# Whole projection units and copied head sums in a woven attention, and a reordered expert loop, in an fp32 two-block transformer

## The chip, the cores and the metric

The kernel runs on one core of one Trainium2 chip. The metric is the device time of one execution in microseconds (us), lower is better. TensorE (PE), VectorE (DVE), ScalarE (ACT) and GpSimd (POOL) each run an instruction stream of their own, SyncE (SP) issues most of the loads; they meet at semaphores only, which the program waits on by hand.

## The reference, cut to what matters

Two transformer blocks follow each other on 1024 tokens of width 1024, all in fp32. The parts that the change touches are the attention of the first block and the expert feed-forward of the second:

```
# first block: 8 heads of 64, three dilated windows mixed
q = rms_norm(q per head, g_q) * 64 ** -0.5
k = rms_norm(k per head, g_k)
y_attn = dilated_mixture(q, k, v)      # causal, scores + a bias, exp, sum, times v
y_conv = gb * short_conv(gc * u, conv_w)
...
# second block: 16 experts, each picks its 130 best tokens of 1040
xs  = u[top_idx]                                            # gather
hid = silu(xs @ w_gate[e]) * (xs @ w_up[e])                 # 1024 -> 512
y   = (hid @ w_down[e]) * top_aff                           # 512 -> 1024
out[top_idx] += y                                           # scatter with add
```

## The kernel before, in words

**First attention.** Heads are handled as four pairs `pp` (0 to 3). For a pair the 1024 queries are 8 tiles of 128; tile t needs one chunk of up to 512 keys (t < 4) or two, so a pair has 12 steps `s`: steps 0 to 3 are tiles 0 to 3, steps 4 and 5 tile 4, and so on to steps 10 and 11 for tile 7. At a step `g = 12 pp + s` PE issues `scores(g + 2)` (two heads, up to 512 columns each), `turn_probs(g, 0)` and `turn_probs(g, 1)` (transposes of the exponentials, up to four for each head), `turn_recips(g - 1)` (one transpose, for a tile's first chunk only) and `values(g - 1)`. DVE takes the turned probabilities of head 0 out of PSUM, adds the bias to the scores and takes the minimum (`scores`), and ACT takes those of head 1, does the exponentials and copies the turned reciprocals (`spread_recips`), on which `values` waits.

Between these PE has the projections of the next pair to do, woven in as units of 24 matmuls of 512 columns (`unit(kind, pp, half, part)`, L1273): at steps 0 and 1 the two halves of k, at 2 and 3 of q, 4 and 5 of v, 6 and 7 of u, then c and b. Pair 0 has no unit at steps 6 and 7, the last pair none from step 6. A unit has two parts of 12 matmuls. All kinds share PSUM banks 2 (half 0) and 3 (half 1), so a unit may start when its bank has been read out (`wait_taken`). The same two banks take the head sums of the squares of k (end of step 3) and of q (end of step 5): `head_sums`, L1288. ACT then reads these banks with a square root (`root_halves`, L793, after an exchange of tables, because it does exponentials in between), and DVE divides (`norm_half`, L1007 and L1009: at steps 4 and 5 for k, 6 and 7 for q). So the v unit of step 4 and the u unit of step 6 wait for ACT's square roots.

```
# wait_taken, before: what the unit behind the head sums waits for
elif before in ("ks", "qs"):
    pe.wait_ge(S["a1_sd"], 2 * norm_index(before[0], of) + half + 1)
```

**Experts.** For each of 16 experts PE multiplies the turned tokens `xsT` by four blocks of `w_gate` and `w_up` (L2838), ACT applies silu, DVE the product (`hidT`, L2389); PE multiplies `hidT` by `w_down` (L2846), DVE copies the result to `yT`; PE turns it back (`yT`, `y_rest`, L543), DVE and ACT weigh it (`y_row_a` L2401, `y_row_b` L1977), POOL scatters it with an add (L1656). Between down and the turning back PE turns the next expert's gathered tokens (`turn_tokens`), which DVE takes out to `xsT` (L2382). The order is written out by hand; the middle experts run in a hardware loop (`Fori`). POOL's loop is gather(e + 1), then scatter(e); SP loads each weight block of the next expert when the block before it has been used.

Of the kernel before, what the change touches and what calls it, by code (L numbers as in the profile page):

```python
# [9 lines left out]
ALU = mybir.AluOpType  # L10
# [140 lines left out]
def build(nc, A, out):  # L151

    ctx = ExitStack()
    with ctx:
# [217 lines left out]
        def thirds(t):  # L372
# [22 lines left out]
            a1_u a1_raw a1_sq a1_ss a1_sd a1_r a1_qn a1_vf a1_vt a1_vs a1_s a1_max a1_e a1_t a1_pt_d a1_pt_a a1_o a1_y a1_rd a1_rl a1_rt a1_rb a1_acc  # L395
# [222 lines left out]
        def wait_taken(pe, kind, pp, half):  # L618
# [4 lines left out]
            elif before in ("ks", "qs"):  # L623
                pe.wait_ge(S["a1_sd"], 2 * norm_index(before[0], of) + half + 1)
# [64 lines left out]
        with nc.Block() as block:  # L689
# [58 lines left out]
            def _(act):  # L748
# [39 lines left out]
                def root_halves(kind, pp, first):  # L788

                    i = norm_index(kind, pp)  # L790
                    for half in range(2):
                        act.wait_ge(S["a1_ss"], 2 * i + 2 if i % 2 else 2 * i + half + 1)
                        act.activation(roots[i % 2][:, half * BANK:(half + 1) * BANK], bank(first + half), ACT.Sqrt, scale=1.0 / HD, bias=eps[:, :]).then_inc(S["a1_sd"], 1)  # L793
# [180 lines left out]
            def _(dve):  # L974
# [25 lines left out]

                def norm_half(kind, pp, half):
# [118 lines left out]
                for g in range(DCT * NS):  # L1120
# [121 lines left out]
            def _(pe):  # L1242
# [254 lines left out]
        with nc.Block() as block:  # L1497
# [99 lines left out]
            def _(pool):  # L1597
# [51 lines left out]
                def scatter(e):  # L1649
# [3 lines left out]
                    for r, (ready, n, to, done) in enumerate((("ex_ra", e * 2 + 2, h_rows, "ex_add_a"), ("ex_rb", e + 1, h_pieces, "ex_add_b"))):  # L1653
                        pool.wait_ge(S[ready], n + CREDIT)
# [9 lines left out]
                with pool.Fori(0, NE - 1) as e:  # L1664
                    pool.wait_ge(S["ex_xt"], e * 3 + 3)
                    gather(e + 1)
                    scatter(e)
# [4 lines left out]
            def _(act):  # L1672
# [294 lines left out]
                act.sem_inc(S["ex_rb"], CREDIT)  # L1967
                with act.Fori(0, NE) as e:
                    for j in range(EK):
                        act.wait_ge(S["ex_g"], e * EK + j + 1)  # L1970
                        act.wait_ge(S["ex_h"], e * EK + j - 1 + 2 * CREDIT)
                        act.activation(silu_e[j % 2][:, :], bank(3 + 2 * (j % 2), CAP), ACT.Silu).then_inc(S["ex_s"], 1)
# [4 lines left out]
                    act.activation(y_row[1][:, :], bank(7, P, 0, PIECES), ACT.Copy, scale=weight[1][:, bass.ds(e, 1)]).then_inc(S["ex_rb"], 1)  # L1977

# [8 lines left out]
            def _(dve):  # L1987
                for n in ("aa_max", "aa_y", "mg_ma", "ex_ra"):
                    dve.sem_inc(S[n], CREDIT)
# [395 lines left out]
                def expert(e, more):  # L2385
                    for j in range(EK):
                        dve.wait_ge(S["ex_s"], e * EK + j + 1)
                        dve.wait_ge(S["ex_u"], e * EK + j + 1)
                        dve.tensor_tensor(hidT[:, j, :], silu_e[j % 2][:, :], bank(4 + 2 * (j % 2), CAP), ALU.mult).then_inc(S["ex_h"], 1)  # L2389
# [5 lines left out]
                    if more:  # L2395
                        take_tokens(e + 1)

                    dve.wait_ge(S["ex_free"], e + CREDIT)
                    for n in range(2):
                        dve.wait_ge(S["ex_r"], e * 3 + n + 2)  # L2400
                        dve.tensor_scalar(y_row[0][:, n * BANK:(n + 1) * BANK], bank(5 + n), weight[0][:, bass.ds(e, 1)], None, ALU.mult).then_inc(S["ex_ra"], 1)  # L2401

                take_tokens(0)
                with dve.Fori(0, NE - 1) as e:
                    expert(e, True)
                expert(NE - 1, False)
# [10 lines left out]
            def _(pe):  # L2417
# [410 lines left out]
                def expert(e, more):  # L2828
                    pe.wait_ge(S["ex_xc"], e * 4 + 4)
                    for j in range(EK):  # L2830
                        if j == 1:
                            pe.wait_ge(S["ex_ra"], e * 2 + CREDIT)
                        if j >= 2:
                            pe.wait_ge(S["ex_h"], e * EK + j - 1 + 2 * CREDIT)
                        for w, b, ld, done in ((w_gate, 3, gate_ld, "ex_g"), (w_up, 4, up_ld, "ex_u")):
                            pe.wait_ge(ld[j], 16 * e + 16)
                            for c in range(KD):
                                last = mm(bank(b + 2 * (j % 2), CAP), w[:, j, c, :], xsT[:, c, :], start=(c == 0), stop=(c == KD - 1))  # L2838
                            last.then_inc(S[done], 1)
                    pe.wait_ge(S["ex_h"], e * EK + EK + 2 * CREDIT)  # L2840
                    pe.wait_ge(S["ex_rb"], e + CREDIT)
# [7 lines left out]
                    if more:  # L2849
                        turn_tokens(e + 1)  # L2850

                    pe.wait_ge(S["ex_yt"], e * 4 + 4)
                    turn(bank(7, P, 0, PIECES), y_rest.rearrange("p c n -> p (c n)")).then_inc(S["ex_r"], 1)
                    for n in range(2):
                        for c in range(4):
                            last = turn(bank(5 + n, P, c * P), yT[:, 4 * n + c, 0:P])
                        last.then_inc(S["ex_r"], 1)
# [62 lines left out]
```

## Time and profile before

| | us |
|---|---|
| median of 3 runs (lowest, highest) | 3569.82 (3563.36, 3573.26) |
| the profiled execution | 3568.07 |
| its span, first to last instruction | 3566.2 |
| PE busy (matmuls) | 3323.8, 93% |
| DVE, ACT, POOL busy | 1402.9, 1033.7, 802.4 |
| mean granted clock of TensorE | 0.967 of full speed |

The profile is of one execution. PE is the engine to watch: the others are busy for less than half of the span. A row names line, engine, operation, `out<-in`, the shape, and in brackets how long the engine sat idle before it and what ended that. PEld is the loading of PE's weights, which runs ahead of its matmuls. An fp32 matmul stands in the trace as two, so a `x16` there is eight instructions.

### The profile page before, as it was taken

How to read it: one execution, taken by the hardware profiler on the slowest of the kernel's cores; microseconds unless marked ns; L12 is line 12 of the kernel's file. 1: busy time of each engine (PE TensorE's matmuls, PEld its weight loads, DVE VectorE, ACT ScalarE, POOL GpSimd, SP SyncE). 2: the span in 40 equal slices, each digit the busy share in tenths (PEclk: the TensorE clock that was granted, in tenths of full speed). 3: DMA queues.
4: the chain of work that ended last, by engine and by line, in shares of the span. 5: the costliest groups of instructions: out<-in, count | busy, mean ns of one | idle time of the engine just before them, and what ended most of it. 6: DMA issues, size and time to landing. Idle time of an engine off the chain costs nothing.

```text
span 3566.2 us, 52694 instructions
## 1 busy us (share of the span) xinstructions
PE 3323.8 (93%) x20576; PEld 2909.0 (82%) x20576; DVE 1402.9 (39%) x2466; ACT 1033.7 (29%) x1888; POOL 802.4 (22%) x513
## 2 busy tenths in 40 slices
PE   7999988999999998999999799899999999689996
PEld 5666766888887887998989689898889999589995
DVE  4544553000002544666666630355455043522222
ACT  4433331000001213555555520155445110301112
POOL 3111123333332333122111133110000223012221
PEclk9999999999999998999999999999999999889998
DMA  3100012111112112000000001300000121468886
GB/s 147 30 30 28 27 72 84 47 47 47 47 47 89 48 53 90 19 19 25 19 19 19 13 26 45 108 25 25 21 23 19 64 101 50 167 225 297 294 305 230
DMA packets 75335, 275.44 MB, mean 77 GB/s; under 512 B 10736, under 2 KB 15600, under 8 KB 74400
## 3 DMA queue, kind: packets, MB, share of 16 engines
q1 hardware_dynamic: 67952, 234.08, 19.1%
q0 software_dynamic: 5632, 17.04, 1.9%
q10 hardware_dynamic: 1584, 22.07, 1.5%
q8 instruction: 108, 1.77, 0.2%
q14 instruction: 59, 0.48, 0.0%
HBM read 229.49 MB, written 38.34 MB: 75 GB/s over the span
## 4 chain that ended last, share of the span: by engine, by line
PE 53%; DVE 3%; issue 3%; ACT 1%; DMA 1%; POOL 0%; SPq 0%; DVEq 0%; ACTq 0%; POOLq 0%
PE PS L555 13%; PE PS L2838 7%; PE PS L2434 6%; PE PS L543 5%; PE PS L2498 3%; PE PS L2846 3%; PE PS L2620 3%; PE PS L2696 3%; PE PS L2465 3%; PE PS L2661 3%; PE PS L2499 0%; PE PS L2778 0%; PE PS L2697 0%; DMA part_b<-raw_b 0%; PE PS L2644 0%
## 5 line engine op out<-in xcount | busy, mean ns | idle before, releaser
L577 POOL CAST w_hi<-ring 128x1024 fp32r<-128x1024 f32 x174 | 183.9, 1057 | 1929.4 <-PE PS L555 772.6
L579 POOL TENSOR_TENSOR w_lo<-ring,w_hi 128x1024 fp32r<-128x1024 f32 x174 | 435.5, 2503 | 14.0
L555 PE MATMUL PS<-u_hi,w_hi 128*128 128x512 f32 (+1 forms) x1256 | 349.0, 369 | 17.8 <-DVE u_lo L509 7.7
L555 PE MATMUL PS<-u_lo,w_hi 128*128 128x512 f32 (+1 forms) x1256 | 351.6, 371 | 0.0
L555 PE MATMUL PS<-u_hi,w_lo 128*128 128x512 f32 (+1 forms) x1256 | 350.4, 370 | 0.0
L555 PEld LDWEIGHTS PS<-u_hi,w_hi 128*128 128x128 f32 x1256 | 228.1, 190 | 58.6 <-issue 12.7
L555 PEld LDWEIGHTS PS<-u_hi,w_lo 128*128 128x128 f32 x1256 | 228.5, 189 | 37.2
L555 PEld LDWEIGHTS PS<-u_lo,w_hi 128*128 128x128 f32 x1256 | 228.8, 189 | 33.2
L1708 ACT ACTIVATE EA<-EA,small_sb 128x1040 f32<-128x1040 f32 x144 | 166.7, 1158 | 209.7 <-DVE small_sb L2047 209.7
L1190 DVE TENSOR_TENSOR hid<-sq,PS 128x1024 f32 x22 | 26.9, 1222 | 457.9 <-PE PS L555 457.9
L2047 DVE CUSTOM_DVE_ANT_0 EA<-PS,biasH,low_a 128x1024 f32<-128x1024 f32 x128 | 163.6, 1278 | 62.5 <-PE PS L2465 62.0
L2434 PE MATMUL PS<-u_hi,w_hi 128*128 128x348 f32 x504 | 173.5, 344 | 0.0
L1273 PE MATMUL PS<-u_hi,w_hi 128*128 128x512 f32 x352 | 148.9, 423 | 16.2 <-ACT sd L793 6.9
L2498 PE MATMUL PS<-Va,PTa 128*128 128x128 f32 (+1 forms) x1152 | 143.5, 279 | 21.8 <-ACT PTa L1716 21.8
L2434 PE MATMUL PS<-u_lo,w_hi 128*128 128x348 f32 x504 | 162.1, 322 | 0.0
L2434 PE MATMUL PS<-u_hi,w_lo 128*128 128x348 f32 x504 | 161.8, 321 | 0.0
L2498 PEld LDWEIGHTS PS<-Va,PTa 128*128 128x128 f32 (+1 forms) x1152 | 135.4, 183 | 27.4 <-ACT PTa L1716 24.9
L1196 DVE TENSOR_TENSOR hid_lo<-hid,hid_hi 128x1024 fp32r<-128x1024 f32 x44 | 94.0, 2177 | 123.9 <-ACT hid_hi L946 123.9
L1273 PE MATMUL PS<-u_lo,w_hi 128*128 128x512 f32 x352 | 141.1, 401 | 0.0
L1273 PE MATMUL PS<-u_hi,w_lo 128*128 128x512 f32 x352 | 140.4, 399 | 0.0
L2696 PE MATMUL PS<-PTb,Vb 128*128 128x128 f32 (+1 forms) x1056 | 130.4, 277 | 0.4 <-DVE obT L2229 0.4
L2838 PE MATMUL PS<-xsT,w_gate_sb 128*128 128x130 f32 x1024 | 128.4, 278 | 1.7 <-DVE xsT L2382 0.7
(402 smaller groups left out, 6753.1 us busy)
## 6 DMA issues: line engine op xcount, KB each, us to landing
ring<-in_stream SPq DMA_DIRECT2D x174, 512.0 KB, 3.6
w_gate_sb<-in_w_gate SPq DMA_DIRECT2D x64, 512.0 KB, 6.4
w_up_sb<-in_w_up SPq DMA_DIRECT2D x64, 512.0 KB, 6.9
w_down_sb<-in_w_down SPq DMA_DIRECT2D x64, 512.0 KB, 5.4
x_keep<-xT ACTq DMA_DIRECT2D x2, 4176.0 KB, 12.8
xT<-x_keep ACTq DMA_DIRECT2D x1, 4176.0 KB, 13.5
x2T<-x_keep ACTq DMA_DIRECT2D x1, 4176.0 KB, 13.0
x_keep<-x2T SPq DMA_DIRECT2D x1, 4176.0 KB, 14.6
```

The source lines that it names most:

```text
L543: return nc.tensor.transpose(out, in_, eye[0:k, 0:k])
L555: last = mm(bank(to_bank, width), w[j][:, c, :], src[:, c, b * width:(b + 1) * width], start=(c == 0 and k == 0), stop=(c == KD - 1 and k ...
L577: pool.tensor_copy(w_hi[j][:, :, :], w_raw[j][:, :, :]).then_inc(S["w_rounded"], 1)
L579: pool.tensor_tensor(w_lo[j][:, :, :], w_raw[j][:, :, :], w_hi[j][:, :, :], ALU.subtract).then_inc(S["w_split"], 1)
L1273: last = mm(bank(2 + half), w[n % 2][:, d, :], src[:, d, half * BANK:(half + 1) * BANK], start=(d == 0 and k == 0), stop=(d == KD - 1 and ...
L1708: act.activation(e[0:m, :], e[0:m, :], ACT.Exp, scale=-1.0, bias=small[0:m, 8 + 2 * par + k:9 + 2 * par + k], accum_out=small[0:m, 12 + 2 ...
L2047: dve.tensor_tensor_reduce(e[0:m, 0:T1], wide(2 * k, T1, m), bias, -1.0, low_a[0:m, t, k:k + 1], ALU.add, ALU.min, low).then_inc(S["aa_max ...
L2434: last = mm(bank(WEAVE, CH), w[slot][:, d, :], src[:, d, columns_of(c)], start=(d == 0 and k == 0), stop=(d == KD - 1 and k == 2))
L2465: last = mm(bank(2 * k + b, BANK, 0, m), q[rows, t * P:t * P + m], keys[rows, b * BANK:(b + 1) * BANK], start=(n == 0), stop=(n == 2))
L2498: mm(bank(7, P, 0, m), PTa[par][:, j, 0:m], Va[:, j, :], start=(j == 0), stop=False)
L2696: mm(bank(7, m), Vb[:, i, :], PTb[s % 2][:, i, 0:m], start=(i == 0), stop=False)
L2838: last = mm(bank(b + 2 * (j % 2), CAP), w[:, j, c, :], xsT[:, c, :], start=(c == 0), stop=(c == KD - 1))
```

## The change

In the first attention:
- a unit is issued whole (24 matmuls). At steps 0, 4 and 6 it stands between `turn_probs(g, 0)` and `turn_probs(g, 1)`, at all others ahead of `scores(g + 2)`;
- DVE copies the head sums out of banks 2 and 3 into the buffers of the roots (`take_sums`, 12 copies of 128x512 in all, for pairs 1 to 3), at the end of steps 3 and 5, ahead of `norm_half`. ACT's square root then works in place, and the next unit waits for DVE's copy (`a1_sc`).

In the experts:
- PE turns the tokens of expert e + 1 between the last gate and up block and down of expert e;
- the result of expert e is turned back, and weighed, after the first gate and up block of expert e + 1, into banks 7, 0 and 1 (before: 7, 5 and 6);
- POOL gathers two experts ahead of the scatter; PE waits for the weighed rows of expert e - 1 ahead of down of expert e.

```
-                pe.wait_ge(S["a1_sd"], 2 * norm_index(before[0], of) + half + 1)
+                pe.wait_ge(S["a1_sc"], 2 * norm_index(before[0], of - 1) + half + 1)
...
+                def take_sums(kind, pp):
+                    i = norm_index(kind, pp)
+                    dve.wait_ge(S["a1_qn"], 2 * (i - 1))
+                    for half in range(2):
+                        dve.wait_ge(S["a1_ss"], 2 * i + 2 if i % 2 else 2 * i + half + 1)
+                        dve.tensor_copy(roots[i % 2][:, half * BANK:(half + 1) * BANK], bank(2 + half)).then_inc(S["a1_sc"], 1)
...
                     if pp + 1 < DCT:
+                        if s in (3, 5):
+                            take_sums("k" if s == 3 else "q", pp + 1)
                         if s in (4, 5):
                             norm_half("k", pp + 1, s - 4)
...
-                    if woven and s:
-                        unit(*woven, 0)
+                    late = s in (0, 4, 6)
+                    if woven and not late:
+                        whole_unit(*woven)
                     if g + 2 < DCT * NS:
                         scores(g + 2)
...
-                    if woven and s == 0:
-                        unit(*woven, 0)
-                    if woven:
-                        unit(*woven, 1)
+                    if woven and late:
+                        whole_unit(*woven)
                     turn_probs(g, 1)
...
+                def expert(e, first, more):
                     pe.wait_ge(S["ex_xc"], e * 4 + 4)
+                    hidden(e, 0)
+                    if not first:
+                        turn_back(e - 1)
+                    for j in range(1, EK):
+                        hidden(e, j)
+                    if more:
+                        pe.wait_ge(S["ex_h"], e * EK + EK - 1 + 2 * CREDIT)
+                        turn_tokens(e + 1)
                     pe.wait_ge(S["ex_h"], e * EK + EK + 2 * CREDIT)
+                    if not first:
+                        pe.wait_ge(S["ex_ra"], e * 2)
+                        pe.wait_ge(S["ex_rb"], e)
```

The instruction order shows where things stand now. First PE in the expert loop of the kernel before; `xs_a` and `xs_b` are the gathered tokens.

```order
L2838 MATMUL PS<-xsT,w_gate_sb 128x130 x8
L2838 MATMUL PS<-xsT,w_up_sb 128x130 x8
L2840 REGISTER_ALU
L2841 REGISTER_ALU
L2842 ISA
L2846 MATMUL PS<-hidT,w_down_sb 128x130 x32
L2819 ISA
L543 MATMUL PS<-eye_sb,xs_a 128x128 x8
L543 MATMUL PS<-eye_sb,xs_b 128x16
L543 MATMUL PS<-eye_sb,y_rest 16x128
L543 MATMUL PS<-eye_sb,yT 128x128 x8
L2860 REGISTER_ALU
```

And PE in the same loop of the changed kernel, from the turning back to the branch's register.

```order
L543 MATMUL PS<-eye_sb,y_rest 16x128
L543 MATMUL PS<-eye_sb,yT 128x128 x8
...
L2873 MATMUL PS<-xsT,w_up_sb 128x130 x8
L2893 REGISTER_ALU
L2858 ISA
L543 MATMUL PS<-eye_sb,xs_a 128x128 x8
L543 MATMUL PS<-eye_sb,xs_b 128x16
L2895 REGISTER_ALU
L2897 REGISTER_ALU
L2899 ISA
L2903 MATMUL PS<-hidT,w_down_sb 128x130 x32
L2909 REGISTER_ALU
```

The nine transposes of tokens have moved from behind down to ahead of it, and those of `yT` from the end of the loop to behind the next expert's first block.

Second, DVE at steps 5 and 6 of pair 0 in the kernel before, from the probabilities of step 5 (`PT_2_92`) on; `sd` holds the roots of k, `E` the exponentials' buffers.

```order
L1072 COPY PT_2_92<-PS 128x128
L1061 ISA E_2_88,small_sb<-PS,bias_98,small_sb 128x256
L1061 ISA E_3_89,small_sb<-PS,bias_98,small_sb 128x256
L1007 RECIPROCAL sd<-sd 128x512
L1009 TENSOR_TENSOR kT_1_82<-kT_1_82,sd 128x512
L1072 COPY PT_0_90<-PS 128x512
L1061 ISA E_0_86,small_sb<-PS,bias_98 128x512
```

And the same place of the changed kernel.

```order
L1084 COPY PT_2_92<-PS 128x128
L1073 ISA E_2_88,small_sb<-PS,bias_98,small_sb 128x256
L1073 ISA E_3_89,small_sb<-PS,bias_98,small_sb 128x256
L1011 COPY sq_71<-PS 128x512 x2
L1019 RECIPROCAL sd<-sd 128x512
L1021 TENSOR_TENSOR kT_1_82<-kT_1_82,sd 128x512
L1084 COPY PT_0_90<-PS 128x512
L1073 ISA E_0_86,small_sb<-PS,bias_98 128x512
```

The two copies of q's head sums stand ahead of the reciprocal for the second half of k, and behind both the work of step 6.

## Rows read from the trace of the kernel before

**Rows 1.** The page: the span.
```profile
span 3566.2 us, 52694 instructions
```

**Rows 2.** The chain that ended last, in one expert (start, us, what).
```profile
3261.39 14.60 PE PS L2838 x128
3276.60 7.42 PE PS L2846 x64
3284.02 2.12 PE PS L543 x18
```

**Rows 3.** Timeline of the same expert: PE's weight loads, and DVE's last take-out.
```profile
3260.85 0.41 DVE L2382 TENSOR_TENSOR xsT<-PS,gains_sb 128x256 f32<-128x256 f32 x1
...
3276.59 7.24 PEld L2846 LDWEIGHTS PS<-hidT,w_down_sb 128*128 128x128 f32 x64 [0.81 <-issue]
...
3284.82 0.13 PEld L543 LDWEIGHTS PS<-eye_sb,xs_b 16*128 16x128 f32 x1 [0.17 <-issue]
...
3286.20 1.86 PEld L2838 LDWEIGHTS PS<-xsT,w_gate_sb 128*128 128x128 f32 x16 [0.31 <-issue]
```

**Rows 4.** Timeline, last expert, outside the loop: the same wait.
```profile
3524.52 7.24 PEld L2846 LDWEIGHTS PS<-hidT,w_down_sb 128*128 128x128 f32 x64 [0.64 <-DVE hidT L2389]
```

**Rows 5.** DMA and waits, 3140 to 3540 us: each queue's share of 16 engines; POOL's wait.
```profile
q1 hardware_dynamic: 26058, 94.88, 64.8%
q0 software_dynamic: 5177, 15.74, 15.8%
...
POOL pick_g_a L1643 <- DMA h_rows<-y_row_b,pick_s_b: 93.6, 13, 7.8
```

**Rows 6.** Line L1273, all units: what ended PE's idle time (us, times).
```profile
  ACT sd L793: 6.9, 3
  ACT sq L793: 6.3, 2
```

**Rows 7.** Windows: the first 12 matmuls after each of these waits (stretch, length, clock).
```profile
123.46:126.41 2.95, 2.95 (x13) 1.00 0.42 161
220.39:224.84 4.45, 4.45 (x13) 0.62 0.24 91
243.89:248.00 4.11, 4.11 (x12) 0.68 0.11 44
333.24:337.75 4.51, 4.51 (x12) 0.62 0.24 93
356.79:361.12 4.33, 4.33 (x13) 0.64 0.12 45
```

**Rows 8.** Timeline at steps 3 and 4 of pair 1.
```profile
216.10 1.98 PE L1288 MATMUL PS<-sq,block_sb 128*128 128x512 f32 x4
216.22 2.35 POOL L579 TENSOR_TENSOR w_lo<-ring,w_hi 128x1024 fp32r<-128x1024 f32 x1
...
216.50 2.23 DVE L1092 TENSOR_TENSOR attn_acc<-attn_acc,y_sq 128x128 f32<-128x128 f32 x1
...
219.56 1.27 ACT L793 ACTIVATE sd<-PS,eps_sb 128x512 f32<-128x512 f32 x2
```

**Rows 9.** Timeline at steps 5 to 7 of pair 0, where no unit is woven.
```profile
138.00 3.35 DVE L1007 RECIPROCAL sd<-sd 128x512 f32<-128x512 f32 x1
...
142.21 1.13 PE L1310 MATMUL PS<-kT,qT 64*128 64x512 f32 x4
...
143.97 0.69 DVE L1072 COPY PT<-PS 128x512 f32<-128x512 f32 x1 [0.54 <-PE PS L543]
...
145.93 0.92 PE L1310 MATMUL PS<-kT,qT 64*128 64x384 f32 x4 [1.19 <-DVE small_sb L1061]
...
147.05 0.27 PE L543 MATMUL PS<-eye_sb,r_rows 128*128 128x128 f32 x1
147.16 0.38 PE L543 MATMUL PS<-eye_sb,E 128*128 128x128 f32 x2
147.69 1.09 PE L1350 MATMUL PS<-PT,V 128*64 128x128 f32 x16
```

More of the change, by code:

```diff
@@ L1965, in _, with hidden, weigh @@
                         act.activation(u_row[t % 2][0:rows, cols], src, ACT.Copy, scale=by_token(3)[0:rows, t:t + 1]).then_inc(S["hr_c"], 1)
[L1967 to L1972, printed above, removed]
+                def hidden(e, j):
+                    act.wait_ge(S["ex_g"], e * EK + j + 1)
+                    act.wait_ge(S["ex_h"], e * EK + j - 1 + 2 * CREDIT)
+                    act.activation(silu_e[j % 2][:, :], bank(3 + 2 * (j % 2), CAP), ACT.Silu).then_inc(S["ex_s"], 1)
+                def weigh(e):
                     act.wait_ge(S["ex_free"], e + CREDIT)
@@ L2394, in expert @@
                     dve.tensor_copy(y_rest[:, :, :], yT[:, :, P:CAP]).then_inc(S["ex_yt"], 1)
[L2395 to L2401, printed above, removed]
-                take_tokens(0)
-                with dve.Fori(0, NE - 1) as e:
-                    expert(e, True)
-                expert(NE - 1, False)
+                take_tokens(0)
+                expert(0, True, True)
+                with dve.Fori(1, NE - 1) as e:
+                    expert(e, False, True)
+                expert(NE - 1, False, False)
+                weigh(NE - 1)
                 dve.wait_ge(S["gfin_ld"], 16)
@@ L2826, in turn_tokens, with hidden @@
                             last.then_inc(S["ex_xt"], 1)
-                def expert(e, more):
-                    pe.wait_ge(S["ex_xc"], e * 4 + 4)
[L2830 to L2839, printed above, removed]
+                def hidden(e, j):
+                    pe.wait_ge(S["ex_h"], e * EK + j - 1 + 2 * CREDIT)
+                    for w, b, ld, done in ((w_gate, 3, gate_ld, "ex_g"), (w_up, 4, up_ld, "ex_u")):
+                        pe.wait_ge(ld[j], 16 * e + 16)
+                        for c in range(KD):
+                            last = mm(bank(b + 2 * (j % 2), CAP), w[:, j, c, :], xsT[:, c, :], start=(c == 0), stop=(c == KD - 1))
+                        last.then_inc(S[done], 1)
@@ new lines, in turn_back, with expert @@
+                def turn_back(e):
+                    pe.wait_ge(S["ex_yt"], e * 4 + 4)
+                    turn(bank(7, P, 0, PIECES), y_rest.rearrange("p c n -> p (c n)")).then_inc(S["ex_r"], 1)
+                    for n in range(2):
+                        for c in range(4):
+                            last = turn(bank(n, P, c * P), yT[:, 4 * n + c, 0:P])
+                        last.then_inc(S["ex_r"], 1)
+                def expert(e, first, more):
+                    pe.wait_ge(S["ex_xc"], e * 4 + 4)
+                    hidden(e, 0)
+                    if not first:
+                        turn_back(e - 1)
+                    for j in range(1, EK):
+                        hidden(e, j)
+                    if more:
+                        pe.wait_ge(S["ex_h"], e * EK + EK - 1 + 2 * CREDIT)
+                        turn_tokens(e + 1)
@@ L2848, in expert @@
                             last.then_inc(S["ex_y"], 1)
[L2849 to L2857, printed above, removed]
-                turn_tokens(0)
-                with pe.Fori(0, NE - 1) as e:
-                    expert(e, True)
-                expert(NE - 1, False)
+                turn_tokens(0)
+                expert(0, True, True)
+                with pe.Fori(1, NE - 1) as e:
+                    expert(e, False, True)
+                expert(NE - 1, False, False)
+                turn_back(NE - 1)
 def layout(inputs):
```

48 lines of the change are left out of this document (35 added, 13 removed).

## The prediction

> **What bounds the kernel now.** I read the page first, then the chain that ended last, then for each of the two stages the weight loads, waits and granted clock of PE.
>
> In the experts PE is the chain. One expert is 14.60 us of gate and up, 7.42 of down and 2.12 of turning [rows 2], 24.14 together, while the first weight load of the next gate follows at 3286.20 [rows 3], 24.81 after the last. So 0.67 of each expert is wait by that reckoning, in which the last matmul of a group counts as busy until it drains. The weight loads show the seams without that drain: they stand idle for 0.81 us ahead of down and for 0.31 ahead of the next gate, 1.12 together [rows 3]. The 0.81 is PE waiting for the last block's silu and product. Outside the loop the same wait is 0.64 [rows 4]; the loop adds register instructions behind it. The 0.31 ends 0.12 us after DVE's last `xsT` piece (3260.85 + 0.41 = 3261.26, load at 3261.39 by [rows 2]): DVE's take-out is the last thing there. DMA is no bound: the queues are busy 64.8% and 15.8% of the stretch, and POOL sits 7.8 us until its scatter has landed with time to spare [rows 5].
>
> In the first attention PE waits for ACT's roots: 6.9 us in three waits ahead of the v unit and 6.3 in two ahead of the u unit [rows 6], so 2.3 and 3.15 each. After four of the five its clock is low: the first 12 matmuls take 2.95 us where the clock is 1.00, and 4.45, 4.11, 4.51 and 4.33 where it is 0.62 to 0.68 [rows 7], which is a stretch at the lower of the two levels (1.2 GHz), then the upper (2.4). That cost 17.40 - 4 x 2.95 = 5.6 us.
>
> **Experts, step by step.** The work of PE is the same instructions; what moves is what stands in the two gaps. The nine transposes of tokens now follow the last up block. They take about half of the 2.12 us, 1.06, and cover the 0.81 for the product: down starts when they are through. They need the banks of block 2, whose product is done a block (3.6 us) before, and gathered tokens, which POOL now asks for nearly a whole expert (24 us) ahead; POOL's landing wait of 7.8 fits in that three times. `xsT` is then ready during down, with 7.42 us of cover, so the 0.31 goes too. The turning back stands behind a block of 3.6 us, which covers DVE's copies; the weighing has three blocks (11 us) before down wants the banks. The new waits of PE ahead of down (weighed rows) end long before. New are two more seams between transposes and matmuls. No row shows one without a wait; between 0 and the 0.17 of the small piece [rows 3], the nearest, I take 0.15 each. So 1.12 - 0.30 = 0.82 per expert. Fifteen experts have it (the last has no tokens to turn): 12.3 us. From both sides: 0.67 less 0.34 gives 5; 1.12 with free seams gives 17. Start and end are unchanged: the last scatter still follows the last weighing. The further copy of an expert's code outside the loop I cost at nothing, as the last expert runs outside it now without a stall beyond [rows 4].
>
> **Attention, gains.** The v unit now waits for DVE's copy, and one step's scores and transposes stand between it and the head sums. The head sums take 1.98 us [rows 8]; a copy of 128x512 out of PSUM costs DVE 0.69 as [rows 9] has it for the probabilities. The first copy is done while the second head sum runs, the second before the scores (1.13) and transposes are through. For q both copies wait for both sums and still end about 1.4 us after them, with scores of 1.13 and four transposes of head 0 ahead of the u unit. I expect all five waits gone: 13.2 us, and the 5.6 of the clock, 18.8 together. A whole unit saves nothing by itself, since the seam from transposes to matmuls was free.
>
> DVE's `attn_acc` add takes 2.23 us for 128 columns [rows 8], just while POOL's 2.35 us subtraction runs and ending with it. The copies stand behind that add, at about the end of the first head sum, and that is late but still covered. The Trainium skill (GPSIMD Engine Reference, 1. Specifications) says that GpSimd shares its SBUF interfaces with VectorE and contends with DVE instructions that have two SBUF inputs; by that rule, the trace agrees, a copy out of PSUM is not held, and copies held as long as the add would put back up to 1 us of each of five waits.
>
> **Attention, losses.** (a) *Pair 0, step 7.* No unit is woven in here. Before, DVE began the second reciprocal of k (3.35 us) at 138.00, ahead of the head sums' end, and PE waited 1.19 us for DVE's scores of step 8 [rows 9]. Now that reciprocal stands behind the two copies. From the end of the head sums (142.21 in the old trace): copies 1.5, reciprocal 3.35, product 0.7, probabilities 0.6, two score operations 1.3, in all 7.5 us with the handing over; PE gets to the next scores after 145.93 - 1.19 - 142.21 = 2.5. The wait grows from 1.2 to about 5.1: 3.9 lost. The clock falls after four of the five waits of 2.3 us or more, so I add one such fall: 1.4. In pairs 1 and 2 a whole u unit (5.9 us) lies there and covers it.
> (b) *Reciprocals.* `values` waits for ACT's copy of the turned reciprocals. From the reciprocals' transpose to the first value matmul this takes 147.69 - 147.05 = 0.64 us where nothing hides it [rows 9]; before, half a unit did in all woven steps. Now only the transposes of head 1 lie there: 0.11 to the first of them (147.05 to 147.16), then about 0.1 for each and 0.1 more. With 1, 2, 3 and 4 of them I get waits of 0.32, 0.22, 0.11 and 0. Steps 1, 2, 3, 5, 7, 9 and 11 have 2, 3, 4, 1, 2, 3 and 4: 0.98 in a pair; without the steps that had no unit before, 3.4 us over four pairs.
> (c) *Step 0* comes after a step whose unit stands ahead of its scores, so scores follow scores within some 2.8 us and DVE needs 3.1: 0.3 in three pairs. In the last pair step 4 has no head sums ahead, 0.4. Together 1.3, an estimate from the same durations.
>
> So attention gains 18.8 - 3.9 - 1.4 - 3.4 - 1.3 = 8.8 us.
>
> **The sum.** 12.3 + 8.8 = 21.1 us. The profiled execution took 3568.07 (span 3566.2 [rows 1]), 1.75 below the median of the runs; 3569.82 - 21.1 = 3548.7, and I say 3548.
>
> **The rivals.**
> *Gains eaten.* The seams of the experts cost what they cost now (5 us gained) and DVE, now with 8.3 us of copies more, is late in pairs 1 and 2 as well. For it: DVE's two reciprocals, products and score operations fill most of steps 5 to 7. Against: the u unit's 5.9 us. Two more waits of 2 us with a fall of clock leave 8.8 - 2 x 3.4 = 2. Time 3569.8 - 7 = 3563, within 0.3%. Chance 0.16.
> *Only one half works.* The experts give their 12 and attention comes out even, because PE then waits at step 3, where the head sum of q's second half needs ACT's square, now with less between: 1.3 us of ACT against the value matmuls. Or attention gives 10 and the experts little. Time 3558, faster by 0.33%. Chance 0.15.
> *All gains, small losses.* Seams free (17), DVE less late in pair 0 and no fall of the clock (13): 3540. Chance 0.13.
> *Slower: the clock.* In the first attention PE is kept at the lower level over many units. What speaks for it: waits of 2.3 us were enough for it in two of three cases [rows 7], and the new order has a wait of 5 us and some twenty small ones. Each unit wholly at half clock costs 5.9 us more (2 x 2.95). It decides from (21.1 + 10.7) / 5.9, five to six of the 40 units; eight would give 3596. Against: after each fall the level is back within the next 12 matmuls or a little later. The Trainium skill (TensorE: Matmul & The Clock Gate, What's actually happening) calls the low clock the default that activity releases; by that rule a stage as dense as this returns to the upper level, and the trace agrees. Chance 0.05.
> The forecast itself has 0.51, with a range of its own of 3542 to 3555.
>
> **How the numbers follow.** A measurement of this kernel tells a change from none at about 0.3%, 10.7 us, so faster is below 3559.1. Forecast, the full-gain case and most of the half case lie there: 0.51 + 0.13 + 0.12 = 0.76. Within: the eaten gains and the rest of the half case, 0.19. Slower 0.05. The range for 8 in 10 takes in the full-gain case and most of the others: 3537 to 3563.
>
> **What would show it.** Right: no idle time of PE's units for ACT's roots; the windows after the head sums of pairs 1 and 2 at clock 1.00; one longer wait of PE for DVE's scores in pair 0 (5 us); short waits of the value matmuls for `r_cols`; an expert period of 24.0 us, with no idle ahead of down except in the last. Wrong: a period above 24.4; PE idle ahead of the v or u unit for DVE's copy; low clock in windows other than pair 0's. The prediction fails if DVE rather than PE sets the steps 5 to 8 of pairs 1 and 2, or if the expert loop finds another wait at its branch.

## The result, and the profile after

| | us | against before |
|---|---|---|
| before, median of 5 runs | 3569.29 (3563.36 to 3573.26) | |
| after, median of 5 runs | 3543.33 (3541.62 to 3548.38) | ratio 0.9931, 95% interval 0.9917 to 0.9946 |
| after, the profiled execution | 3545.09, span 3543.3 | 22.9 off the span of [rows 1] |

The medians differ by 26.0 us, the ratio stands for 24.6. 3548 was forecast, with a range of 3537 to 3563. To see where the time went, I cut each span at events that exist in both kernels (the first start of a line's matmuls, read from that line's rows).

| stretch | before | after | difference |
|---|---|---|---|
| first attention: first unit to the first L555 matmul | 466.8 | 455.8 | -11.0 |
| second attention: first `EA` transpose to the last woven unit | 559.0 | 565.4 | +6.4 |
| the rest from L555 to the first gate matmul | 2049.8 | 2049.0 | -0.8 |
| experts: first gate matmul to the end | 431.3 | 414.4 | -16.9 |

The four add up to 22.3; the first unit also starts 0.6 earlier. The second row was not in the forecast: the diff leaves the second attention alone. Each row is read from one execution. Over all fourteen profiles of this study the untouched third row varies from 2044.1 to 2054.1, so a few us there mean nothing, while the second attention takes between 559.0 and 559.4 us in four of them.

**Experts.** PE's weight loads in the changed kernel, from the turning back to down (start, length, instruction, and in brackets idle time before it):

```profile
3204.87 0.36 PEld L543 LDWEIGHTS PS<-eye_sb,yT 128*128 128x128 f32 x3
3205.20 1.87 PEld L2873 LDWEIGHTS PS<-xsT,w_gate_sb 128*128 128x128 f32 x16
...
3214.15 1.87 PEld L2873 LDWEIGHTS PS<-xsT,w_up_sb 128*128 128x128 f32 x16
3215.94 0.91 PEld L543 LDWEIGHTS PS<-eye_sb,xs_a 128*128 128x128 f32 x8
3217.02 0.13 PEld L543 LDWEIGHTS PS<-eye_sb,xs_b 16*128 16x128 f32 x1 [0.17 <-issue]
3217.18 5.00 PEld L2903 LDWEIGHTS PS<-hidT,w_down_sb 128*128 128x128 f32 x44
```

The 0.81 and 0.31 of [rows 3] are gone. The seams from transposes to gate, from up to transposes and from transposes to down carry no bracket at all; the 0.17 ahead of the small piece was there before. Down follows down after 23.70 us, where it was 24.81:

```profile
3217.18 7.43 PE L2903 MATMUL PS<-hidT,w_down_sb 128*128 128x130 f32 x64
3240.88 7.43 PE L2903 MATMUL PS<-hidT,w_down_sb 128*128 128x130 f32 x64
```

**First attention.** What PE waited for from 58 to 445 us, after (total us, times, longest):

```profile
PE PS L1324 <- DVE small_sb L1073: 5.8, 2, 4.8
PE PS L1287 <- POOL w_lo L579: 2.3, 1, 2.3
PE PS L1364 <- issue: 0.8, 4, 0.2
PE PS L1364 <- ACT r_cols L860: 0.8, 3, 0.3
PE PS L1287 <- ACT V L821: 0.7, 3, 0.2
```

ACT's roots of [rows 6], 13.2 us in five waits, are no longer in the list. The long wait is in pair 0, where DVE does the copies (L1011) first:

```profile
139.96 1.29 DVE L1011 COPY sq<-PS 128x512 f32<-128x512 f32 x2 [2.46 <-PE PS L1302]
141.16 3.34 DVE L1019 RECIPROCAL sd<-sd 128x512 f32<-128x512 f32 x1
144.54 0.69 DVE L1021 TENSOR_TENSOR kT<-kT,sd 128x512 f32<-128x512 f32 x1
145.15 0.68 DVE L1084 COPY PT<-PS 128x512 f32<-128x512 f32 x1
145.75 0.68 DVE L1073 CUSTOM_DVE_ANT_0 E<-PS,bias 128x512 f32<-128x512 f32 x1
```

DVE sits idle for 2.46 us until the head sums are there; in that time it would have done most of the reciprocal. PE meanwhile:

```profile
147.10 1.65 PE L1324 MATMUL PS<-kT,qT 64*128 64x384 f32 x4 [4.81 <-DVE small_sb L1073]
...
149.95 1.97 PE L1364 MATMUL PS<-PT,V 128*64 128x128 f32 x16
151.85 0.78 PE L1287 MATMUL PS<-u_hi,w_hi 128*128 128x512 f32 x1
```

The score matmuls (x4) take 1.65 us, where they took 0.92, and the value matmuls (x16) 1.97, where they took 1.09 [rows 9]: PE is at its lower level. The windows (stretch, length, busy time of PE, PEld, DVE, ACT, POOL, then the granted clock, the DMA share and GB/s) say where; in the first the v unit of pair 1 begins, at 223.05, behind its head sums; [rows 7] had 0.62 there:

```profile
220.00:225.00 5.00, 5.00 (x22) 2.80 (x21) 4.38 (x9) 4.84 (x10) 0.92 (x1) 1.00 0.38 105
...
147.10:151.85 4.75, 4.75 (x25) 3.00 (x25) 4.68 (x7) 2.25 (x4) 0.00 (x0) 0.50 0.02 3
```

0.50 is the lower level (1.2 GHz) throughout.

The list of waits ends at 445 us, shortly behind the start of the last woven unit (443.6). Up to that start the stage is 13.1 us shorter than before; from there to the first L555 matmul it is 2 us longer (70.9 against 68.9). There the changed kernel has the granted clock at half from 456.3 to 466.5 us, where the kernel before has one such stretch of 3.4 us (from 467.3). No run settles where that comes from: `attention_alone` (below), with the same attention, has 3.4 us of it.

**Second attention.** DVE at a turn of the loop over the heads, whose code is the same in both kernels, after:

```profile
1655.49 0.18 DVE L2070 COPY EA<-meta_a 128x16 f32<-128x16 f32 x1 [3.83 <-issue]
1658.05 1.28 DVE L2073 CUSTOM_DVE_ANT_0 EA<-PS,biasH,low_a 128x1024 f32<-128x1024 f32 x1 [2.38 <-issue]
```

And the same two instructions of the kernel before:

```profile
1664.30 0.17 DVE L2044 COPY EA<-meta_a 128x16 f32<-128x16 f32 x1 [4.02 <-PE PS L543]
1664.57 1.28 DVE L2047 CUSTOM_DVE_ANT_0 EA<-PS,biasH,low_a 128x1024 f32<-128x1024 f32 x1
```

A gap of about 4 us stands ahead of the first instruction in both. The 2.38 behind it is new, has no releaser ("issue"), and comes twice, at both turns of the loop (2.38 and 2.22). Together they are 4.6 us, while the stage is 6.4 longer. PE's own idle time in the stage goes from 7.7 to 9.5 us, and its granted clock is at half for 10.2 us, where the kernel before has none. `experts_alone` and `before_9_more` (below) have 6.8 us of the lower level at the same turns and yet take 559.3 and 559.0 us, so that much of it didn't lengthen the stage; how idle time and clock share the rest isn't shown. Which edit brings the gap was the first question.

### The profile page after: what moved, and what is told of

Its sections match the earlier page's. It is cut to its first block, busy times and chain, and to the rows that moved or that the text cites. A ratio compares the mean times of both kernels' runs of the same rounds, so it can differ in the third digit from the quotient of the medians.

```text
span 3543.3 us, 52696 instructions
## 1 busy us (share of the span) xinstructions
PE 3316.2 (94%) x20576; PEld 2909.4 (82%) x20576; DVE 1389.7 (39%) x2478; ACT 1013.7 (29%) x1873; POOL 801.4 (23%) x513
## 4 chain that ended last, share of the span: by engine, by line
PE 52%; DVE 4%; issue 3%; ACT 1%; DMA 1%; POOL 0%; SPq 0%; DVEq 0%; ACTq 0%; POOLq 0%
PE PS L555 13%; PE PS L2873 7%; PE PS L2473 6%; PE PS L543 5%; PE PS L2537 3%; PE PS L2659 3%; PE PS L2903 3%; PE PS L2735 3%; PE PS L2504 3%; PE PS L2700 3%; PE PS L2538 0%; PE PS L2817 0%; PE PS L2736 0%; PE PS L2683 0%; DMA part_b<-raw_b 0%
## 5 line engine op out<-in xcount | busy, mean ns | idle before, releaser
L555 PE MATMUL PS<-u_hi,w_hi 128*128 128x512 f32 (+1 forms) x1256 | 352.5, 372 | 17.1 <-DVE u_lo L509 7.7
L555 PE MATMUL PS<-u_lo,w_hi 128*128 128x512 f32 (+1 forms) x1256 | 352.2, 371 | 0.0
L555 PE MATMUL PS<-u_hi,w_lo 128*128 128x512 f32 (+1 forms) x1256 | 349.3, 369 | 0.0
L555 PEld LDWEIGHTS PS<-u_hi,w_hi 128*128 128x128 f32 x1256 | 229.1, 190 | 55.2 <-issue 12.3
L555 PEld LDWEIGHTS PS<-u_hi,w_lo 128*128 128x128 f32 x1256 | 229.2, 190 | 37.7
L555 PEld LDWEIGHTS PS<-u_lo,w_hi 128*128 128x128 f32 x1256 | 229.7, 190 | 35.8
L2089 DVE SCALAR_TENSOR_TENSOR EA<-EA,small_sb,EA 128x1040 f32<-128x1040 f32 (+1 forms) x72 | 126.9, 1762 | 2.6
```

The costliest lines, as they stand in the source:

```text
L555: last = mm(bank(to_bank, width), w[j][:, c, :], src[:, c, b * width:(b + 1) * width], start=(c == 0 and k == 0), stop=(c == KD - 1 and k ...
L2089: dve.scalar_tensor_tensor(EA[par][0:m, :], EA2[0:m, :], c2, EA[par][0:m, :], ALU.mult, ALU.add).then_inc(S["aa_c"], 1)
```

## The experiments

All ratios are against the kernel before, with their 95% intervals. Stage lengths are read as in the table above.

**The two halves apart.** `experts_alone` is the kernel before with the expert part of the diff, `attention_alone` with the attention part.

> The kernel before with the change of the expert loop only; the attention stage is as before. Theory A (the three parts of the kernel add up, and the 5.6 us or more that the trace after loses between the first attention and the router, where no code was changed, is variation between executions): the experts save what the two traces show, 24.81 - 23.70 = 1.11 us for each of 15, and with the start and end of the stage 17.5 us; ratio 0.9951, about 3552 us, and the stretch from the first L555 weight load to the first gate is that of before within 3 us. Rival B (the expert part loses something elsewhere, for instance by a longer first or last expert, or by its code): less than 14 us saved, and the unchanged stretch is longer here too.

> The kernel before with the whole units and the copies of the head sums only; the expert loop is as before. Theory A: the first attention saves 11.6 to 13 us (its last unit ends 13.6 us earlier in the trace after), nothing is given back between it and the router, and the whole is 3557 to 3558 us, ratio 0.9966. Rival B: an earlier or other end of the attention shifts the phase in which the clock or the weight queues stand in the next stage, 5.6 to 8 us are given back there in every execution, and the whole is 3563 to 3565 us, ratio 0.9985, with the stretch from the first L555 weight load to the first gate longer by 5 us or more than in the kernel before.

`experts_alone`: 3553.00 us, ratio 0.9954 (0.9941 to 0.9967), 17.1 us off the median of before; experts 414.5 us; second attention 559.3. Theory A stands.

`attention_alone`: 3560.53 us, ratio 0.9975 (0.9965 to 0.9984), 9.6 us off. Neither side had this time. First attention 456.0 and experts 432.2, as A says, but the second attention takes 566.0 us. So it gives back some 6 us, by B's size, and in the attention half of the diff; the two halves together (26.7) are the whole (26.0).

**The attention part split.** `order_only` has PE's new order and no copies, `copies_only` the copies and PE's old order:

```
 # order_only: all of the attention part that is taken
-                    if woven and s:
-                        unit(*woven, 0)
+                    late = s in (0, 4, 6)
+                    if woven and not late:
+                        whole_unit(*woven)
...
-                    if woven and s == 0:
-                        unit(*woven, 0)
-                    if woven:
-                        unit(*woven, 1)
+                    if woven and late:
+                        whole_unit(*woven)
```

> The kernel before with PE's order of the change in the first attention alone: whole units, late at steps 0, 4 and 6. The head sums still go from PSUM to ACT's square root, and the units still wait for it; the expert loop is as before. Theory A (the order covers most of the wait by itself, the copy the rest): scores and four transposes, 1.7 us, now lie between the head sums and the unit, so that 0.6 us of each 2.3 and 1.4 of each 3.15 remain, 4.6 us in place of 13.2; with the clock's 5.6 back and the small waits of 3.3 (measured after: 1.9 and 0.8 for r_cols, and up to 1 for scores) it saves 10 to 11 us, and pair 0 keeps its short wait of 1.2 us at step 7. Rival B (the copy does the work, because it is DVE and not ACT that comes first): waits of 1.5 us or more remain in all five places, the clock stays low behind them, and the gain is under 4 us.

> The kernel before with the head sums copied out by DVE, and PE's old order of half units in the first attention; the expert loop is as before. Theory A: a unit follows the head sums at once and waits for the first copy, 0.7 us and the handing over, 0.9 to 1.2 us in five places instead of 2.3 and 3.15; the clock's 5.6 us come back, and pair 0 has its wait of 4.8 us at step 7 and one fall of the clock: 13.2 - 5 + 5.6 - 3.6 - 1.4 = about 9 us saved. Rival B (DVE reaches the copies late, because the attn_acc add of 2.23 us beside POOL's subtraction stands ahead of them): waits of 2 us and more remain for k, the clock is low behind them, and less than 4 us are saved.

`order_only`: 3555.60 us, ratio 0.9968 (0.9959 to 0.9977), 13.4 us off the median; first attention 454.0, second 559.4. What is left of the waits, 58 to 445 us:

```profile
PE PS L1273 <- ACT sq L793: 2.7, 2, 1.4
...
PE PS L1310 <- DVE small_sb L1061: 2.2, 2, 1.2
PE PS L1273 <- ACT sd L793: 2.1, 3, 0.7
```

These are 4.8 us of waits for ACT's roots in place of 13.2, as Theory A had it (4.6), and no window of 5 us between 60 and 445 is below 1.00: waits of 0.7 and 1.4 us left the clock up. By medians the order alone gains more than the whole attention part does (13.4 and 9.6), though the intervals of the two ratios overlap.

`copies_only`: 3566.24 us, ratio 0.9996 (0.9987 to 1.0005): no difference. Its waits:

```profile
PE PS L1324 <- DVE small_sb L1073: 5.8, 2, 4.8
PE PS L1287 <- DVE sd L1011: 4.2, 3, 1.4
...
PE PS L1287 <- DVE sq L1011: 2.3, 2, 1.3
```

PE waits 6.5 us for the copies, where Theory A had 5. The first attention takes 460.0, 7 to 11 less than in the kernels with its old form (466.8 to 470.9), which is Theory A's size for the stage. The second attention takes 564.1, which gives most of it back. So what lengthens the second attention comes with the copies, not with the order.

**Code place or copies?** The copies put 18 instructions into DVE's stream ahead of the second attention. `before_18_more` puts 18 others there and nothing else (36 waits, of which two go into one instruction), `before_9_more` 9 (18 waits):

```
                 dve.memset(gated[:, 0:2], 0.0).then_inc(S["conv_a"], 1)
                 dve.wait_ge(S["bias_ld"], 16)
+                for _ in range(36):
+                    dve.wait_ge(S["bias_ld"], 16)
```

> The kernel before, nothing of the change, with 18 more instructions in DVE's stream at its start: waits that are already satisfied, put where DVE stands idle for 19 us until ACT's first root. DVE's loop over the heads of the second attention then stands at instructions 1158 to 1542 of its stream, in place of 1140 to 1524 (of the changed kernel: 1157 to 1541). Why: the kernels with the copies have two stalls of 2.4 us in DVE at the start of a turn of this loop, ahead of L2073 with no releaser, and the stage takes 562 to 565 us against 559 in the kernels without copies. Theory A (the place of the code in DVE's stream is the cause): the stalls of 2.4 us appear here too, the stage from the first EA transpose to the last woven unit takes 563 to 565 us, and the whole is 5 to 6 us slower than before, ratio 1.0015. Rival B (the copies or the earlier end of the first attention are the cause, not the code's place): no stall, 559 us, the time of the kernel before. The Trainium skill (Runtime: NRT & Kernel Launch, Instruction fetch mechanics) says that an engine other than PE holds two blocks of 256 instructions and that a taken branch to a block not held waits for a fetch; by that rule the loop of 384 instructions fits into two blocks when it stands at 1140 and not at 1158.

> As the kernel before with 18 more instructions in DVE's stream, but with 9 only: the loop over the heads stands at 1149 to 1533. Theory A1 (what counts is whether the loop passes a certain place in the stream, which lies between a shift of 9 and one of 18): no stall of 2.4 us, stage 559 us, time of the kernel before. Theory A2 (any shift against the lucky place of before costs, or the certain place lies within the first 9): stalls as with 18, 5 to 6 us slower. Rival B: no stall with either. By the rule of the Trainium skill (Runtime: NRT & Kernel Launch, Instruction fetch mechanics) the end of the second block is instruction 1536 if the stream is counted from its first instruction, and A1 follows.

`before_18_more`: 3573.52 us, ratio 1.0012 (1.0004 to 1.0021), 4.7 us slower; second attention 564.1. `before_9_more`: 3568.75, ratio 0.9999 (0.9991 to 1.0008); second attention 559.0. DVE at the same turn of the loop, first with 18:

```profile
1666.48 0.17 DVE L2046 COPY EA<-meta_a 128x16 f32<-128x16 f32 x1 [4.15 <-issue]
1668.94 1.28 DVE L2049 CUSTOM_DVE_ANT_0 EA<-PS,biasH,low_a 128x1024 f32<-128x1024 f32 x1 [2.29 <-issue]
```

And with 9, where the second gap is absent:

```profile
1666.36 0.18 DVE L2046 COPY EA<-meta_a 128x16 f32<-128x16 f32 x1 [3.94 <-issue]
```

Theory A with A1: instructions added ahead of the loop make the stall by themselves, and whether they do turns between a shift of 9 and one of 18. By the rule of the Trainium skill (Runtime: NRT & Kernel Launch, Instruction fetch mechanics) that both expectations name, so it should be.

**Moving the loop on.** `after_130_more` is the changed kernel with 260 such waits at the same place, that is 130 instructions; `best_130_more` is `late_sums_recips` (below) with the same.

> The changed kernel with 130 more instructions of the same kind at the same place of DVE's stream, so that the loop over the heads stands at 1287 to 1671. They take some 8 us of DVE's 19 us of idle time. Theory A: the two stalls of 2.4 us go, the stage from the first EA transpose to the last woven unit takes 559 us in place of 565, and the whole is 5 to 6 us shorter than the changed kernel, about 3538. Rival B: no change of the stage, 3543 us; or, if the padding is on the path, up to 8 us slower.

> The kernel with the late copies of q's sums in pair 0 and the reciprocals turned first (3537.6 us median, 448.0 us of first attention), with the same 130 instructions more in DVE's stream. Theory A: the stage of the second attention takes 559 us, and the whole is 5 to 6 us shorter, 3532 us, ratio 0.9905. Rival B: 3537 us as without them.

`after_130_more`: 3545.67 us, ratio 0.9931 (0.9919 to 0.9943), second attention 565.8; `best_130_more`: 3540.81 us, ratio 0.9920 (0.9908 to 0.9932), second attention 565.4. Nothing gained. The stall has not gone but moved into the first gap, in `after_130_more`:

```profile
1658.17 0.17 DVE L2072 COPY EA<-meta_a 128x16 f32<-128x16 f32 x1 [6.13 <-issue]
```

6.13 is about the 4 and the 2.3 of the other kernels in one. So Theory A's cure failed. The rule of the Trainium skill (Runtime: NRT & Kernel Launch, Instruction fetch mechanics), two held blocks of 256, with the blocks counted from the stream's start (a loop from 1287 to 1671 lies in two), gave the step between 9 and 18 and not this; here the measurement decides. That the place matters is shown; which places are good is not, beyond the ones tried, and that fetching is the mechanism isn't shown either.

**Pair 0.** `late_sums` is the changed kernel with the copies of q's head sums of pair 0 a step later in DVE's order:

```
                     if pp + 1 < DCT:
-                        if s in (3, 5):
+                        if s == 3 or s == 5 and pp:
                             take_sums("k" if s == 3 else "q", pp + 1)
                         if s in (4, 5):
                             norm_half("k", pp + 1, s - 4)
+                        if s == 6 and not pp:
+                            take_sums("q", pp + 1)
```

> The changed kernel, with the copies of q's head sums of pair 0 moved in DVE's order from the end of step 5 to step 6, behind the scores of step 8, so that the second reciprocal of k no longer stands behind them. Theory A (the 4.81 us wait of PE in pair 0 is the price of that order): the wait falls to 1.0 to 1.7 us, the low clock of the two windows 145 to 155 goes, and the attention stage is 3.5 to 5 us shorter than in the changed kernel: about 3539 us against 3543. Rival B: DVE is short of time over steps 5 to 8 as a whole, so that the wait comes back at the scores of step 9 or 10, behind the reciprocals of q: less than 1.5 us saved.

3539.37 us, ratio 0.9920 (0.9907 to 0.9933), 4.0 below the median of the changed kernel, whose interval it overlaps. The first attention takes 453.9 us, 1.9 less than after and not the 3.5 to 5 of Theory A. PE in pair 0:

```profile
143.96 0.92 PE L1326 MATMUL PS<-kT,qT 64*128 64x384 f32 x4 [1.20 <-DVE small_sb L1073]
...
147.50 1.98 PE L1366 MATMUL PS<-PT,V 128*64 128x128 f32 x16 [1.93 <-ACT r_cols L860]
```

The 4.81 is 1.20, as Theory A said, but a new wait of 1.93 begins 1.6 us after its end, ahead of the value matmuls. The clock is low all the same: 0.50 from 146.9, within that wait, to 153.7 us, and the value matmuls (x16) take 1.98 us. ACT shows why:

```profile
145.27 1.33 ACT L797 ACTIVATE sq<-sq,eps_sb 128x512 f32<-128x512 f32 x2 [2.81 <-DVE sq L1011]
...
147.19 0.26 ACT L860 ACTIVATE r_cols<-PS 128x128 f32<-128x128 f32 x1
```

ACT takes its work in the order of its stream. Its roots of q still stood at the end of step 5; it now sat idle for 2.81 us until their input was there, and `r_cols` was queued behind them. I had moved the copy and not its consumer; the version that moves both was not run. Add PE's wait for the scores and the time from its end to the next unit. That is 1.20 + 5.45 us here (the unit's first matmul starts at 149.41), 4.81 + 4.75 in the changed kernel and 1.19 + 2.79 in the kernel before (148.72).

`late_sums_recips` also turns the reciprocals ahead of both heads:

```
+                    if g and chunks[(g - 1) % NS][1] == 0 and not late:
+                        turn_recips(g - 1)
                     turn_probs(g, 0)
-                    if g and chunks[(g - 1) % NS][1] == 0:
+                    if g and chunks[(g - 1) % NS][1] == 0 and late:
                         turn_recips(g - 1)
```

> As the run with the late copies of q's head sums in pair 0, and also the transpose of the reciprocals stands ahead of both heads' transposes of the probabilities in the steps whose unit comes first. Theory A (value matmuls wait for r_cols because only one head's transposes cover ACT's copy): the 1.9 us of waits and 0.8 us of issue gaps ahead of the value matmuls fall to under 0.7 us, and 1.5 to 2.5 us are saved beyond the other run. Rival B: the transpose of the reciprocals now waits itself, for DVE's r_rows or for the result of the step before: PE idle with r_rows or yT as the releaser, and nothing saved or up to 3 us lost.

3537.59 us, ratio 0.9919 (0.9906 to 0.9932). Of the waits for `r_cols` only the 1.9 of pair 0 is left (3.0 us in five before this edit), and the 0.8 us of issue gaps are gone, which is Theory A. The first attention takes 448.0 us, 5.9 less than without this edit; that is more than the 1.9 us that went, and the rest isn't explained. The medians differ by only 1.8, with runs from 3534 to 3548, so the edit's gain in the whole time isn't settled. It is the fastest median of the study, 5.7 below the changed kernel's. The two kernels with the 130 instructions differ in the same two edits: 3540.81 against 3545.67 us, and 449.7 against 456.0 us of first attention.

**The two moves of the experts apart.** `tokens_ahead_only` turns back right behind down, `back_late_only` turns the tokens behind down (both from the changed kernel; DVE's `take_tokens` moves with it in the second):

```
 # tokens_ahead_only
-                    hidden(e, 0)
-                    if not first:
-                        turn_back(e - 1)
-                    for j in range(1, EK):
+                    for j in range(EK):
                         hidden(e, j)
...
                         if c in (2, 5, 7):
                             last.then_inc(S["ex_y"], 1)
+                    turn_back(e)
...
-                turn_back(NE - 1)
 # back_late_only
-                    if more:
-                        pe.wait_ge(S["ex_h"], e * EK + EK - 1 + 2 * CREDIT)
-                        turn_tokens(e + 1)
                     pe.wait_ge(S["ex_h"], e * EK + EK + 2 * CREDIT)
...
                             last.then_inc(S["ex_y"], 1)
+                    if more:
+                        turn_tokens(e + 1)
```

> The changed kernel with the turning back of each expert again right behind its down, and the tokens of the next expert still turned ahead of down. Theory A (the two moves only pay together: in the old order the tokens' transposes were the cover of DVE's copies of yT): PE waits behind down for the last copy of yT (0.41 us), y_rest (0.18) and their handing over, 0.9 to 1.2 us, less than that if it counts from the drained matmul; the expert period is 24.6 to 24.9 us, as before the change, and the whole is 3556 to 3561 us. Rival B (the 0.81 ahead of down was the whole loss and the rest of the 1.11 a seam): the period is 24.0 us and the whole 3548.

> The changed kernel with the tokens of the next expert again turned behind down, and the results still turned back a block into the next expert. Theory A: the wait of 0.81 us ahead of down is back, and the gate matmuls now wait for xsT, because nothing lies between the tokens' transposes and them while DVE first copies yT (0.5 and 0.2 us) and then takes four pieces (1.5 us): 1.0 to 1.4 us. The expert period is 25.5 to 25.9 us and the whole 3571 to 3577 us, slower than the kernel before. Rival B: DVE's pieces keep up with the transposes, the wait for xsT stays at 0.3 us, the period is 24.8 and the whole 3560.

`tokens_ahead_only`: 3557.68 us, ratio 0.9972 (0.9960 to 0.9984), period 24.60 us. Its waits of PE from 3140 to 3540 us:

```profile
PE PS L543 <- DVE y_rest L2438: 11.7, 16, 0.7
PE PS L2900 <- DVE hidT L2415: 0.5, 1, 0.5
```

`back_late_only`: 3578.01 us, ratio 1.0030 (1.0019 to 1.0040), period 26.02 us:

```profile
PE PS L2873 <- DVE xsT L2408: 18.6, 15, 1.3
PE PS L2900 <- DVE hidT L2415: 11.3, 16, 0.8
```

Theory A both times, the second a little worse than expected. Turning the tokens ahead alone brings 0.21 us per expert, turning back late alone costs 1.21, and both together bring 1.11. Each group of transposes was the cover of DVE's work for the other: alone, the first move leaves 0.73 us of waiting for `y_rest` per expert, the second 1.24 for `xsT` and 0.7 for `hidT`.

## Why the prediction was right, and where it was not

The time lay 5 us below the forecast, in its range, and faster by 0.69%, beyond the 0.3% bound. Of the terms:

- **Experts, 12.3 forecast.** 16.9 came (17.1 by medians, alone). The mechanism held: both gaps went, DVE, POOL and DMA kept up (the queues' shares are 67.1% and 17.3%), the last expert kept its wait of 0.5. The mis-sized term is "two more seams between transposes and matmuls", taken as 0.15 each from the 0.17 of the small piece; they cost 0. The same prediction calls such a seam free in the attention. The period fell by 1.11, not 0.82, and 15 x 1.11 is 16.7. The bound above, 17, was the right end.
- **Waits for ACT's roots, 13.2, and clock, 5.6.** Both came whole: none of the five waits is left, and the windows behind them have 1.00. But I gave the credit to the copy. `order_only` removes 8.4 of the 13.2 and all of the clock's part, since the waits that stay are at most 1.4 us. The copy adds the last 4.8, and costs 5.6 in pair 0 (next point) and some 6 in the second attention.
- **(a) Pair 0, 3.9 + 1.4 forecast.** It measured 4.81 - 1.19 = 3.6 for the wait, and 4.75 - 2.79 = 2.0 for the clock, together 5.6.
- **(b) Reciprocals, 3.4.** Over the whole stage the value matmuls wait 1.9 us for `r_cols` in five waits and 0.8 in four issue gaps, 2.7 in all (0.8 + 0.8 up to 445 us).
- **(c) Scores behind scores, 1.3.** No loss shows: without the long one, waits for DVE's scores are 1.0 up to 445 us and were 1.3 before (2.5 with the 1.2).
- **The held copies.** The copies of pair 1 take 1.28 for two, as planned. In the new order POOL's subtraction (218.55 to 220.92 us) no longer meets the `attn_acc` add, which takes 0.28 in place of 2.23, but the copy of the reciprocals ahead of it, 1.35 us where it took 0.23 before (at 213.41). DVE's work out of PSUM keeps its time: the `PT` copy across the subtraction's start takes 0.69 (at 218.31), and a score operation of 128x128 inside it 0.34 (218.92), as outside it in the kernel before (212.68). The two copies of head sums behind the held one, at 221.32 and 221.93, were still done before the v unit began without a wait at 223.05. The held copy:

```profile
219.65 1.35 DVE L1097 COPY r_rows<-small_sb 128x128 f32<-128x128 f32 x1
```

- **What is missing.** The net of the attention, 8.8, looks right against 9.6 measured alone, and is right by luck. The first attention gained more: 11.0 between the two profiles, 13.4 between the means of the profiles with the old form (466.8, 470.9, 469.3 and 469.6) and with the new (455.8, 456.0, 456.2, 454.5 and 456.0). Some 6 us went in the second attention. The step that failed is the count of what each edit adds: I costed the copies' 0.69 us and the code of one more expert, but never asked what 18 more instructions do to the code behind them. `before_18_more` shows what they do alone: 5 us of that stage and 4.7 of the whole.

The stage gains of the first attention sum to less in my terms (18.8 - 5.6 - 2.7 = 10.5) than the 13.4 of the means; the rest is within what the kernels with the old form differ among themselves, 4 us, and I can't place it.

Of the signs named beforehand, the expert period was 23.70 us where 24.0 was named. "Low clock in windows other than pair 0's" was to be a sign of being wrong, and it came: not behind the head sums, but behind the last unit (10.2 us at half) and at the turns of the second attention (10.2 us).

Of the rivals, *all gains, small losses* named the free seams, and 3540 was 3 off. *Slower: the clock* asked for five to six units at half clock; up to the last unit there was less than one. *Only one half works* and *gains eaten* did not come.

## What to carry to other kernels

When an edit adds instructions to an engine's stream, cut both traces at common events and look at the stages that the edit does not touch: a loop behind it may have changed its place in the stream, and the gaps named "issue" at its turn show it. If a consumer waits for a result, first put other work between the two: here the order alone gave at least as much as the whole change of the attention, and the copy, which removed the last 4.8 us of waiting, cost 5.6 in pair 0 and 5 to 7 in the second attention. When a step is moved on one engine, move the in-order neighbour that feeds on it too, or it holds everything queued behind.

## What the runs showed of the hardware

- The place of a loop in DVE's instruction stream changed its time: shifts of 0, -1 and 9 instructions give 559.0 to 559.4 us for the second attention (four kernels), shifts of 17, 18 and 147 give 563.8 to 566.0 (ten kernels). The stall is 2.2 to 2.5 us at each of two turns, on top of a gap of 3.7 to 4.2 that the kernels without it have too; with 147 there is one gap of 6.1 to 6.6 in place of the two. The Trainium skill (Runtime: NRT & Kernel Launch, Instruction fetch mechanics) says that a taken branch whose target block is not held stalls for its fetch. The gaps at the turn agree in kind. The section's two blocks of 256 instructions agree with shifts of 9 and 18 and not with 147. What decides is open.
- In the first attention waits of 0.7, 1.2 and 1.4 us left PE's clock at the upper level (`order_only`). With a wait of 1.20 us, 1.6 us of work and a wait of 1.93, it fell within the second (`late_sums`).
- In the expert loop the seams between fp32 transposes and matmuls of different weights cost nothing measurable (no brackets in the weight loads at 3205.20, 3215.94 and 3217.18 us).
- Beside POOL's subtraction DVE's 128x128 add took 2.23 us for 0.28 and its copy of the reciprocals 1.35 for 0.23, both from SBUF to SBUF. Its reciprocal of 128x512 (3.35) and what it read from PSUM kept their time.
